# Context projections spread over both layers' experts: 8 in layer 0's, 18 in layer 1's

## The chip, the cores and the metric

The kernel runs on one core of a Trainium2 chip. Its engines are TensorE (PE), VectorE (DVE), ScalarE (ACT), GpSimd (POOL) and SyncE (SP), each with its own instruction stream, and sixteen DMA engines bring the data. The metric is the device time of one execution, in microseconds (us); lower is better. All arithmetic is fp32.

## The reference

Two parts follow each other on 256 tokens of width 1024. The first is two layers (l = 0, 1) of a mixer with three branches and a mixture of 64 experts. The second starts with a mixer of four mLSTM heads and a multi-scale pool, which also sees 256 context tokens, and ends with window attention. Cut to what the change touches:

```python
def first_block(x, ...):
    for l in range(2):
        h = rms_norm(x, norm_mix_g[l]) * (1.0 + sc_m) + sh_m
        x = x + g_m * mixer(h, ...)
        h = rms_norm(x, norm_ffn_g[l]) * (1.0 + sc_f) + sh_f
        x = x + g_f * moe_ffn(h, ...)              # 64 experts and a shared one

def second_block(x, c, ctx, c_ctx, ...):           # layer 0 of it
    shift, scale, gate = jnp.split(silu(c) @ w_mod + b_mod, 3)
    shift_c, scale_c, gate_c = jnp.split(silu(c_ctx) @ w_mod + b_mod, 3)
    hx = rmsnorm(x, g_pre) * (1 + scale) + shift
    hc = rmsnorm(ctx, g_pre) * (1 + scale_c) + shift_c
    ux, uc = hx @ w_in, hc @ w_in                  # q, k, v, o, z (4 heads each), pool in and gate (4 groups each), 16 gates
    qx, kx, vx, gates = mlstm_inputs(ux, ...)      # short_conv of width 3 over q and k
    qc, kc, vc, gates = mlstm_inputs(uc, ...)      # scans over log_i, log_f forward and backward
```

`hc` and `uc` depend on the context and on the modulation vectors alone, not on the first part's result.

## The kernel before

The stages stand one after another in the program. For each layer: a norm and the input projections, the branches, the merge of the branches, the routing, then the experts; after both layers the pools of the second part, its four heads, and its attention. Each stage is a Python generator per engine (`pe_...`, `act_...`, `dve_...`, `pool_...`) that emits the instructions of that engine in a fixed order and yields the event that it waits for. A generator `scan` (L2693 on PE, L2719 on ACT, L2764 on DVE) is woven into the pools by `step(scan)`: each `yield PAUSE` in it, and each count of `pause(n)`, hands control back to the pools for one step.

All weights come through one list, `K.loads`. SP issues it in order (L562 to L577): it waits for the events that a load's place needs, then issues the DMA. Nothing further down the list is issued while it waits. The ring has 11 units of 1 MB (`UNITS`, L20). `places` (L364) assigns the loads of the experts to places: ring slots of two units for `up` (w1 and w3, 2 MB), halves of one unit and the places `x`, `consts` and `last` for `down` (w2, 1 MB), and two `wide` places outside the ring. In layer 0 there are four slots, two halves and place `x` (the memory of `K.gate_a`, which is also that of `K.hc`); in layer 1 three slots and four halves, since `K.hc` holds the normed context there.

The experts take 25 passes (`ORDER`, L29): a pass handles one, two or four experts' tokens, PE multiplies by `up` (L2164), scatters the slots of tokens, multiplies by `down` (L2199) and adds the result to the rows (L2215). `pe_fill` (L2220) adds after a pass of layer 1 one context projection: 16 matmuls of 128x256, whose weights (1 MB of `ab_w_in`) come through the same queue as kind `fill`; `act_fill` copies the 128x512 result into `K.turns`, and `pool_experts` writes it to `ctx_parts` in DRAM. `FILL` lists 18 of them: the pools' input and gate for groups 1 to 3, and v, o and z of the four heads. They are read back before the heads and the pools. The heads' q and k have their context part computed in the second part: `pe_project` (L2990) multiplies by `K.h2`, which holds the context's 256 columns and the tokens' 256 columns, at 128x512.

The context is loaded at the start of layer 1, its norm's sums are made by ACT there (`act_ctx_sums`, L919), and `pool_ctx`, `pe_ctx` (L1747) and `act_ctx` turn it and write `K.hc` beside the branches and the merge of layer 1. Modulation vectors are products of one row with a weight (`pe_mod`, L693): `early_parts` and `EARLY_AT` say which stand behind which input projection. The names `mod2` are those of the second part, and all six (q, j) stand in layer 1's projections.

The scans of the gates run in the pools. For each direction d, DVE makes the scans, PE turns the result (`ecol`, L2714 and L2715, eight small transposes) and ACT copies it into `acol` and `ecol`, which the heads read. ACT starts with direction 1 (L2735) only after the turn of direction 0.

## Time and profile before

| | us |
|---|---|
| three timed runs: median (lowest, highest) | 2498.92 (2497.47, 2500.92) |
| the profiled execution | 2502.77 |
| its span in the profile | 2501.4 |
| layer 0: experts | 408.1 to 871.2 |
| layer 1: start, experts | 871.2, 1278.4 to 1817.3 |
| second part: pools, heads | 1817.3 to 1948.5, to 2212.2 |

The span is the time from the first to the last instruction in the trace; 1.4 us of the profiled execution lie around it. A matmul of fp32 operands appears as two records in the trace, so 16 matmuls are "x32". A row of a timeline tells start, duration, engine, line, operation, output and inputs, and in brackets how long the engine was idle before and for what. "cst", "xT", "ar" and "ring" are places of a weight. PEclk is the granted TensorE clock as a share of full speed. The share of a stage that PE idles is not the price of what it waits for elsewhere: look at each stage by itself.

### The profile page before, as it was taken

Reading aid. Unit: us, or ns where it says so; the run is one execution under the profiler, and the core shown is the slowest. Engines: PE = TensorE matmul, PEld = TensorE weight load, DVE = VectorE, ACT = ScalarE, POOL = GpSimd, SP = SyncE. Lnnn points to the kernel's source line nnn. Section 1 sums busy time; section 2 is a strip of 40 time slices with the busy share of each in tenths; the row PEclk is TensorE's granted clock in tenths of the full one; section 3 lists DMA queues with packets and bytes.
Section 4 is the critical chain, followed back from the end, with each engine's and each line's share of the span. In section 5 each row is a group of like instructions: output and inputs, shape, how many; then the busy total and the mean of one; then the engine's idle time right before and its main releaser. Section 6 shows DMA issues by size and latency. Waiting matters only on the chain.

```text
span 2501.4 us, 29863 instructions
## 1 busy us (share of the span) xinstructions
PE 2334.9 (93%) x11723; PEld 1498.8 (60%) x11723; DVE 848.1 (34%) x2148; ACT 560.1 (22%) x1199; POOL 116.2 (5%) x168
## 2 busy tenths in 40 slices
PE   7999999888888889999999899999997999999998
PEld 4867886344334357678855555555565566654764
DVE  0596523122122115955241221212115233321254
ACT  2224311111111121243111111111123233221264
POOL 4000000000000001100000000000000000001110
PEclk9999999999989999999999999999988999999999
DMA  9644665999999898547569999999951532130500
GB/s 342 244 169 168 253 274 214 421 421 421 421 421 421 352 379 298 180 160 277 232 251 399 414 387 407 415 399 414 388 170 50 164 97 80 68 126 12 190 1 18
DMA packets 196905, 657.70 MB, mean 263 GB/s; under 512 B 13617, under 2 KB 66073, under 8 KB 147089
## 3 DMA queue, kind: packets, MB, share of 16 engines
q1 hardware_dynamic: 191024, 645.33, 66.6%
q0 software_dynamic: 5296, 10.32, 1.3%
q8 instruction: 97, 1.59, 0.3%
q14 instruction: 56, 0.45, 0.1%
q10 hardware_dynamic: 432, 0.01, 0.0%
HBM read 649.58 MB, written 6.04 MB: 262 GB/s over the span
## 4 chain that ended last, share of the span: by engine, by line
PE 82%; DMA 11%; DVE 4%; ACT 1%; issue 1%; SPq 1%; POOL 0%; DVEq 0%; ACTq 0%
PE ps L275 46%; PE ps L2164 12%; PE ps L2199 7%; DMA ring<-in_w 4%; DMA cst<-in_w 3%; PE ps L2215 3%; DMA xT<-in_w 3%; PE ps L1747 2%; PE ps L1205 1%; PE ps L3434 1%; PE ps L693 1%; DVE ar L1344 1%; DMA ring<-in_w_in 1%; PE ps L2825 1%; DMA ring<-in_w_mod 1%
## 5 line engine op out<-in xcount | busy, mean ns | idle before, releaser
L275 PE MATMUL ps<-hT,ring 128*128 128x256 f32 (+2 forms) x2352 | 602.9, 413 | 1.9 <-ACT ar L1565 1.9
L275 PEld LDWEIGHTS ps<-hT,ring 128*128 128x128 f32 (+1 forms) x2352 | 445.2, 192 | 150.4 <-issue 94.4
L2164 PE MATMUL ps<-ring,ar 128*32 128x512 f32 (+2 forms) x1184 | 300.5, 618 | 10.9 <-DMA ring<-in_w 5.6
L2164 PE MATMUL ps<-ar 128*64 128x512 f32 (+1 forms) x864 | 265.5, 615 | 13.3 <-DMA ring<-in_w 13.3
L2199 PE MATMUL ps<-ring,ar 128*32 128x512 f32 (+2 forms) x672 | 182.9, 664 | 49.5 <-DMA cst<-in_w 21.6
L2164 PEld LDWEIGHTS ps<-ring,ar 128*32 128x32 f32 (+2 forms) x1184 | 93.1, 128 | 156.7 <-issue 153.5
L2447 DVE TENSOR_TENSOR ar<-ar,ps 128x256 f32<-128x256 f32 x50 | 21.1, 421 | 472.7 <-ACT ar L2307 472.7
L275 PE MATMUL ps<-ring,ar 128*128 128x512 f32 x320 | 139.8, 593 | 0.9 <-DVE ar L3663 0.9
L2471 DVE SCALAR_TENSOR_TENSOR exact_parts<-ps,ar,exact_parts 128x512 fp32r<-128x512 f32 x100 | 75.1, 751 | 193.1 <-ACT exact_parts L2315 187.3
L2164 PEld LDWEIGHTS ps<-ar 128*64 128x64 f32 (+1 forms) x864 | 74.5, 126 | 98.5 <-issue 97.8
L2315 ACT ACTIVATE exact_parts<-ps,ar 128x512 fp32r<-128x512 f32 x100 | 68.7, 687 | 284.0 <-PE ps L2199 260.6
L2199 PEld LDWEIGHTS ps<-ring,ar 128*32 128x32 f32 (+2 forms) x672 | 53.0, 136 | 126.5 <-issue 122.5
L2199 PE MATMUL ps<-cst,ar 128*64 128x512 f32 (+1 forms) x216 | 113.0, 672 | 9.0 <-DMA xT<-in_w 6.6
L2215 PE MATMUL ps<-exact_parts 128*128 128x512 f32 x400 | 108.6, 411 | 2.1 <-DVE exact_parts L2471 2.1
L275 PE MATMUL ps<-exact_parts,exact_rows 128*128 128x256 f32 x832 | 104.1, 282 | 0.0
L2215 PEld LDWEIGHTS ps<-exact_parts 128*128 128x128 f32 x400 | 71.5, 188 | 54.4 <-issue 33.0
L275 PEld LDWEIGHTS ps<-ring,ar 128*128 128x128 f32 x320 | 60.4, 190 | 72.6 <-issue 70.5
L2307 ACT ACTIVATE ar<-ps 128x256 f32<-128x256 f32 x50 | 19.2, 384 | 376.0 <-PE ps L2164 376.0
L275 PEld LDWEIGHTS ps<-exact_parts,exact_rows 128*128 128x128 f32 x832 | 98.6, 189 | 5.1 <-issue 5.0
L1344 DVE SCALAR_TENSOR_TENSOR ar<-ar,wdw 128x256 f32<-128x256 f32 x240 | 101.0, 492 | 0.0
L275 PE MATMUL ps<-ring,hT 128*128 128x256 f32 (+1 forms) x384 | 100.0, 417 | 0.0
L275 PE MATMUL ps<-ar,ring 128*128 128x256 f32 (+1 forms) x416 | 98.7, 397 | 0.6 <-ACT ar L1699 0.6
(453 smaller groups left out, 2789.2 us busy)
## 6 DMA issues: line engine op xcount, KB each, us to landing
ring<-in_w SPq DMA_DIRECT2D x232, 1024.0 KB, 16.4
ar<-in_w SPq DMA_DIRECT2D x108, 1024.0 KB, 14.5
ring<-in_w_mod SPq DMA_DIRECT2D x36, 2048.0 KB, 11.9
ring<-in_w_in SPq DMA_DIRECT2D x28, 2048.0 KB, 12.2
ring<-in_ab_w_in SPq DMA_DIRECT2D x46, 1024.0 KB, 12.4
cst<-in_w SPq DMA_DIRECT2D x27, 1024.0 KB, 18.7
xT<-in_w SPq DMA_DIRECT2D x17, 1024.0 KB, 20.4
ring<-in_w_out SPq DMA_DIRECT2D x4, 2048.0 KB, 11.2
```

Of the source, the lines that this page charges most:

```text
L275: ins = te.matmul(o, l, r, start=(first and i == 0), stop=(last and i == len(pairs) - 1), skip_group_check=lax)
L693: ins = te.matmul(b[32 * t:32 * t + 32, :], col(2 * t + s), w[:, 2 * t + s, :], start=(s == 0), stop=(s == 1))
L1205: ins = te.matmul(b[:, :], h[:, kk, i * P:(i + 1) * P], w[0][:, kk, :], start=(kk == 0), stop=(kk == 7))
L1344: ins = ve.scalar_tensor_tensor(K.acc[:, c, :], K.hpad[:, c, k:k + 256], tap, K.acc[:, c, :], ALU.mult, ALU.add)
L1747: ins = te.matmul(b[:, 0:256], w[kk // 4][:, kk % 4, k::8], K.merged[:, kk, :], start=(kk == 0), stop=(kk == 7))
L2164: ins = te.matmul(b[cols, :], K.x_b[:, kk, in_pair(p, cols)], weights_up(K, l, r)[:, :, kk, :], start=(kk == 0), stop=(kk == 7))
L2199: ins = te.matmul(b[cols, :], K.t_b[:, j * P + cols.start:j * P + cols.stop], weights_down(K, l, r, j, q), start=(j == 0), stop=(j == 1))
L2215: ins = te.matmul(K.banks[2 * i + q][:, :], K.wT_r[:, p % 2, i * P:(i + 1) * P], part[:, q * 512:(q + 1) * 512], start=False, stop=False, ...
L2315: ac.activation(K.o_hi_r[:, q * 512:(q + 1) * 512], K.ps["down", l, p, q][:, :], ACT.Copy, scale=K.slot[:, p, 1:2]).then_inc(*K.act("o_hi" ...
L2471: ve.scalar_tensor_tensor(K.o_lo_r[:, cols], K.ps["down", l, p, q][:, :], K.slot[:, p, 1:2], K.o_hi_r[:, cols].bitcast(F32), ALU.mult, ALU ...
L2825: ins = te.matmul(b[:, cols], w[:, kk, c * P:(c + 1) * P], h[:, kk, cols], start=(kk == 0), stop=(kk == 7))
L3434: ins = te.matmul(b[:, 0:256], w[:, kk, (n % 2) * P:(n % 2 + 1) * P], hx[:, kk, :], start=(kk == 0), stop=(kk == 7))
```

## The change

- `FILL` gets q and k of the four heads: 26 entries. `FILL_OF` divides them: the first eight (the six pool pieces, q and k of head 0) in layer 0, in passes 3, 4, 5, 8, 10, 12, 15 and 18; the other 18 in layer 1, in the passes that had one before.
- The heads' q and k products become 128x256 (the tokens' columns alone); the context's half comes back from `ctx_parts` by a new load of 512 KB per head (`ctx_qk`), and ACT copies it ahead of each of the four pieces.
- `K.hc` is made in layer 0: the load of the context, `act_ctx_sums` (now at the end of layer 0's projections), `pool_ctx`, `pe_ctx` and `act_ctx` move there, and with them the modulation parts mod2 (0, 0) and (0, 1), behind `qk`. Layer 0's experts then have three slots and four halves, and place `x` is gone. POOL writes `K.hc` to DRAM in layer 0's experts, and a new load `hc` of 1 MB brings it back ahead of layer 1's experts. The sines and cosines in `K.turns` are also written out and brought back.
- The scans: PE's `pause(5)` becomes `pause(7 - d)`, ACT's `pause(4)` becomes `pause(6 - d)`.

```diff
@@ -32,10 +32,12 @@
 CONSTS_PASS = 20
-FILL = [(n, g) for g in range(1, 4) for n in ("pin", "pgate")] + [(n, hd) for hd in range(4) for n in ("v", "o", "z")]
-FILL_COL = {"pin": 5, "pgate": 6, "v": 2, "o": 3, "z": 4}
-FILL_PASS = [p for p in range(3, 24) if ORDER[p] > 1 and p != 13]
-FILL_AT = {p: n for n, p in enumerate(FILL_PASS)}
+FILL = [(n, g) for g in range(1, 4) for n in ("pin", "pgate")] + [(n, hd) for hd in range(4) for n in ("q", "k", "v", "o", "z")]
+FILL_COL = {"pin": 5, "pgate": 6, "q": 0, "k": 1, "v": 2, "o": 3, "z": 4}
+FILL_OF = range(8), range(8, 26)
+FILL_PASS = dict(zip(FILL_OF[0], (p for p in range(2, 24) if ORDER[p] > 2 or p in (3, 10, 22))))
+FILL_PASS |= dict(zip(FILL_OF[1], (p for p in range(3, 24) if ORDER[p] > 1 and p != 13)))
+FILL_AT = [{FILL_PASS[n]: n for n in of} for of in FILL_OF]
@@ -314,6 +317,8 @@
     K.cosT, K.sinT = K.turns[:, 0:256], K.turns[:, 256:512]
+    K.turns_kept = nc.dram_tensor("turns_kept", (P, 512), F32).ap()
+    K.hc_kept = nc.dram_tensor("hc_kept", (P, 2048), F32).ap()
@@ -364,15 +369,13 @@
-    slots = 4 if l == 0 else 3
-    up = {("wide", 0): (-1, None), ("wide", 1): (-1, None), **{("slot", n): (-1, None) for n in range(slots)}}
-    down = {(name, 0): (-1, None) for name in (("x", "consts", "last") if l == 0 else ("consts", "last"))}
-    down |= {("half", u): (-1, None) for u in range(10 - 2 * slots)}
+    up = {("wide", 0): (-1, None), ("wide", 1): (-1, None), **{("slot", n): (-1, None) for n in range(3)}}
+    down = {("consts", 0): (-1, None), ("last", 0): (-1, None), **{("half", u): (-1, None) for u in range(4)}}
...
-        fill = [FILL_AT[p]] if l == 1 and p in FILL_AT else []
+        fill = [FILL_AT[l][p]] if p in FILL_AT[l] else []
@@ -435,7 +438,7 @@
-            ("up", pass_of), ("down", pass_of), ("fill", range(len(FILL)) if l == 1 else ()))]
+            ("up", pass_of), ("down", pass_of), ("fill", FILL_OF[l]))]
@@ -444,9 +447,9 @@
-        if l == 1:
-            wide[1].append(("mod", *early_parts(l)[-1]))
-        first = {"wide": wide, "x": [("merged", l, 0, 7)], "consts": [("ctx_turned", 3)] if l else []}
+        wide[1].append(("mod", *early_parts(l)[-1]))
+        kind, r = K.where[0]["consts"]
+        first = {"wide": wide, "consts": [("used", kind, 0, r)] if l else [("ctx_turned", 3)]}
@@ -477,10 +480,6 @@
     for l in range(LAYERS):
-        if l == 1:
-            K.plan(("ctx",), 1, [(lambda f: f.rearrange("p (i d) -> p i d", i=2),
-                                  I["ctx_2"][0].rearrange("(i p) d -> p i d", p=P))],
-                   (K.cst_place, [("used", "down", 0, K.where[0]["consts"][1])]))
@@ -488,6 +487,9 @@
                     mod(*key)
+        if l == 0:
+            K.plan(("ctx",), 1, [(lambda f: f.rearrange("p (i d) -> p i d", i=2),
+                                  I["ctx_2"][0].rearrange("(i p) d -> p i d", p=P))], (K.cst_place, []))
@@ -500,6 +502,9 @@
         shared(l)
+        if l == 1:
+            K.plan(("hc",), 1, [(lambda f: f, K.hc_kept)],
+                   (K.hc.rearrange("p k t -> p (k t)"), [("merged", 1, 0, 7), ("hc_kept",)]))
@@ -511,8 +516,8 @@
-            if n == "v":
-                ctx_parts(("ctx_head", h), FILL.index(("v", h)), 3)
+            if n in ("q", "v"):
+                ctx_parts(("ctx_qk" if n == "q" else "ctx_head", h), FILL.index((n, h)), 2 if n == "q" else 3)
@@ -718,8 +723,8 @@
     if l == 0:
-        return [("mod", 0, j) for j in range(2, 4)]
-    return [("mod2", q, j) for q in range(2) for j in range(3)]
+        return [("mod", 0, 2), ("mod2", 0, 0), ("mod2", 0, 1), ("mod", 0, 3)]
+    return [("mod2", 0, 2), ("mod2", 1, 0), ("mod2", 1, 1), ("mod2", 1, 2)]
@@ -731,19 +736,19 @@
-EARLY_AT = ("qc", "vc"), ("norm", "va", "ua", "ug", "qc", "qk")
+EARLY_AT = ("qc", "qk", "qk", "vc"), ("ua", "ug", "qc", "qk")
...
-def pe_mod(K, key):
+def pe_mod(K, l, key):
...
-        K.te.wait_ge(*(yield ("cact2",)))
+        K.te.wait_ge(*(yield ("cact2", l)))
@@ -948,8 +953,8 @@
     ac = K.ac
-    ac.wait_ge(*(yield ("scales2", 0)))
-    ac.wait_ge(*(yield ("merged", 1, 0, 7)))
+    ac.wait_ge(*(yield ("ctx_scale",)))
+    ac.wait_ge(*(yield ("merged", 0, 0, 7)))
@@ -1269,17 +1274,15 @@
     ac = K.ac
+    for q in range(2):
+        ac.activation(K.cact2[:, :, q * 16:(q + 1) * 16],
+                      K.cact[:, 1 + q, :].unsqueeze(2).to_broadcast([P, 8, 16]), ACT.Copy).then_inc(*K.act())
+    K.act.also("cact2", l)
...
-        for q in range(2):
-            ac.activation(K.cact2[:, :, q * 16:(q + 1) * 16],
-                          K.cact[:, 1 + q, :].unsqueeze(2).to_broadcast([P, 8, 16]), ACT.Copy).then_inc(*K.act())
-        K.act.also("cact2")
...
-    if l == 1:
-        yield from act_ctx_sums(K)
@@ -1328,6 +1331,8 @@
     yield from act_mod_early(K, l, "vc")
+    if l == 0:
+        yield from act_ctx_sums(K)
@@ -1366,6 +1371,8 @@
         at += 14
+    if l == 1:
+        ve.wait_ge(K.s_turns, 32)
@@ -1392,7 +1399,7 @@
-BEFORE_ROPE = (1, 5)
+BEFORE_ROPE = (1, 3)
@@ -1400,6 +1407,12 @@
     yield from pool_mods(K, l, 0, BEFORE_ROPE[l])
+    if l == 0:
+        gp.wait_ge(*(yield ("sin",)))
+        gp.wait_ge(*(yield ("cos",)))
+        gp.dma_start(K.turns_kept, K.turns[:, :]).then_inc(K.s_turns, 16)
+    else:
+        gp.wait_ge(K.s_turns, 32)
@@ -1691,6 +1704,8 @@
     for br, kept in enumerate((K.gate_a, K.gate_b)):
+        if br == 0 and l == 1:
+            K.ac.wait_ge(*(yield ("hc_kept",)))
@@ -1734,7 +1749,7 @@
             yield from pe_direct(K, l, (3 + br,))
-        if br == 1 and l == 1:
+        if br == 1 and l == 0:
@@ -1763,7 +1778,7 @@
     yield from act_direct(K, l, (3, 4))
-    if l == 1:
+    if l == 0:
@@ -1782,6 +1797,9 @@
             dve_scales2(K, 0)
+        if br == 1 and l == 0:
+            dve_scale(K, K.sc2[0][:, 0, :], K.mods2[0][:, 0, 1, :], K.gpre[0])
+            K.dve.also("ctx_scale")
@@ -1815,7 +1833,7 @@
 def pool_branches(K, l):
-    if l == 1:
+    if l == 0:
@@ -2217,23 +2235,27 @@
-def pe_fill(K, n):
+def pe_fill(K, l, n):
...
-    w = k_major(K.flat["fill", 1, n], 256)
+    w = k_major(K.flat["fill", l, n], 256)
...
-    te.wait_ge(*(yield ("ring", "fill", 1, n)))
+    te.wait_ge(*(yield ("ring", "fill", l, n)))
+    if n == FILL_OF[l][0]:
+        te.wait_ge(*(yield (("ctx_h", 7), ("ring", "hc"))[l]))
...
-    K.pe.also("used", "fill", 1, n)
+    K.pe.also("used", "fill", l, n)
...
+    if n == 0:
+        K.ac.wait_ge(K.s_turns, 16)
@@ -2280,8 +2302,8 @@
         yield from pe_down(K, l, p)
-        if l == 1 and p in FILL_AT:
-            yield from pe_fill(K, FILL_AT[p])
+        if p in FILL_AT[l]:
+            yield from pe_fill(K, l, FILL_AT[l][p])
@@ -2314,8 +2336,8 @@
-        if l == 1 and p in FILL_AT:
-            yield from act_fill(K, FILL_AT[p])
+        if p in FILL_AT[l]:
+            yield from act_fill(K, FILL_AT[l][p])
@@ -2473,14 +2495,25 @@
 def pool_experts(K, l):
+    gp = K.gp
...
-        return
-    for n, p in enumerate(FILL_PASS):
-        if p == CONSTS_PASS:
+        gp.wait_ge(*(yield ("ctx_h", 7)))
+        gp.dma_start(K.hc_kept, K.hc.rearrange("p k t -> p (k t)")).then_inc(K.s_hc, 16)
+        K.ev["hc_kept",] = (K.s_hc, 16)
+    late = l == 1
+    for n in FILL_OF[l]:
+        if late and FILL_PASS[n] >= CONSTS_PASS:
...
-        K.gp.wait_ge(*(yield ("ctx_part", n)))
-        K.gp.dma_start(K.ctx_parts[:, n * 512:(n + 1) * 512], K.turns[:, :]).then_inc(K.s_parts, 16)
-    K.ev["ctx_parts_kept",] = (K.s_parts, 16 * len(FILL))
+            late = False
+        gp.wait_ge(*(yield ("ctx_part", n)))
+        gp.dma_start(K.ctx_parts[:, n * 512:(n + 1) * 512], K.turns[:, :]).then_inc(K.s_parts, 16)
+    if late:
+        yield from late_consts(K)
+    if l == 0:
+        gp.wait_ge(K.s_parts, 16 * len(FILL_OF[0]))
+        gp.dma_start(K.turns[:, :], K.turns_kept).then_inc(K.s_turns, 16)
+    else:
+        K.ev["ctx_parts_kept",] = (K.s_parts, 16 * len(FILL))
@@ -2707,7 +2740,7 @@
     for d in range(2):
-        yield from pause(5)
+        yield from pause(7 - d)
@@ -2738,7 +2771,7 @@
-        yield from pause(4)
+        yield from pause(6 - d)
@@ -2793,7 +2826,7 @@
         te.wait_ge(*(yield ("ring", name, 0)))
-        te.wait_ge(*(yield ("ctx_h", 7)))
+        te.wait_ge(*(yield ("ring", "hc")))
@@ -2944,7 +2977,7 @@
     K.gp.wait_ge(*(yield ("y_turned", 1, 7)))
-    K.gp.wait_ge(*(yield ("ctx_h", 7)))
+    K.gp.wait_ge(*(yield ("ring", "hc")))
@@ -2992,8 +3025,8 @@
         K.te.wait_ge(*(yield ("ring", n, hd)))
-    products(K.te, b[:, :], [(w[:, kk, c * P:(c + 1) * P], K.h2[:, kk, :])
-                             for kk in range(8)]).then_inc(*K.pe("m_ps", n, hd, c, ps=b))
+    products(K.te, b[:, 0:256], [(w[:, kk, c * P:(c + 1) * P], K.h2[:, kk, 256:512])
+                                 for kk in range(8)]).then_inc(*K.pe("m_ps", n, hd, c, ps=b))
@@ -3110,17 +3143,21 @@
     for hd in range(4):
+        ac.wait_ge(*(yield ("ring", "ctx_qk", hd)))
...
-                ac.wait_ge(*(yield ("m_ps", n, hd, c)))
...
-                ac.activation(K.upad[:, :, 1:257], segments(K.ps["m_ps", n, hd, c][:, :]),
+                at = (512 if n == "k" else 0) + c * 256
+                ac.activation(K.upad[:, 0, 1:257], K.flat["ctx_qk", hd][:, at:at + 256], ACT.Copy).then_inc(*K.act())
+                ac.wait_ge(*(yield ("m_ps", n, hd, c)))
+                ac.activation(K.upad[:, 1, 1:257], K.ps["m_ps", n, hd, c][:, 0:256],
...
+        K.act.also("used", "ctx_qk", hd)
```

TensorE, the scans' turns in the pools, before (L2825 is the product of a group's input, the products of L275 with 128x256 are its gate, with 128x512 the pool mix; L2714 opens a turn):

```order
L2825 MATMUL ps<-hT,ring 128x256 x16
L275 MATMUL ps<-ar,ring 128x512 x4
L2714 MATMUL ps<-cst,ar 128x4
...
L2715 MATMUL ps<-cst,ar 128x4
L275 MATMUL ps<-hT,ring 128x256 x16
L2825 MATMUL ps<-hT,ring 128x256 x16
L275 MATMUL ps<-ar,ring 128x512 x4
L2714 MATMUL ps<-cst,ar 128x4
```

The same place after (line numbers are 3 or 33 higher there):

```order
L2858 MATMUL ps<-hT,ring 128x256 x16
L278 MATMUL ps<-ar,ring 128x512 x4
L278 MATMUL ps<-hT,ring 128x256 x16
L2858 MATMUL ps<-hT,ring 128x256 x8
L2747 MATMUL ps<-cst,ar 128x4
...
L2748 MATMUL ps<-cst,ar 128x4
L2858 MATMUL ps<-hT,ring 128x256 x8
L278 MATMUL ps<-ar,ring 128x512 x4
L278 MATMUL ps<-hT,ring 128x256 x16
L2858 MATMUL ps<-hT,ring 128x256 x16
L2747 MATMUL ps<-cst,ar 128x4
```

The first turn moved behind a gate product and half an input product; between the turns stand 40 matmuls of 128x256 and four of 128x512, against 32 and four before.

ScalarE, the end of layer 0's projections and the first instructions of its branches, before:

```order
L1329 ACTIVATE ar<-ps 128x512 x2
L775 ACTIVATE ar<-ps 128x512 x2
L1653 ACT_TABLE_LOAD
L1455 ACTIVATE ar<-ar 128x128 x2
L1552 ACTIVATE ar<-ar 128x384 x2
```

and after:

```order
L1332 ACTIVATE ar<-ps 128x512 x2
L780 ACTIVATE ar<-ps 128x512 x2
L924 ACTIVATE xT,par<-cst 128x1024 x2
L927 ACT_TABLE_LOAD
L927 ACTIVATE par<-par,cst 128x2
L929 ACT_TABLE_LOAD
L929 ACTIVATE par<-par 128x2
L1666 ACT_TABLE_LOAD
L1468 ACTIVATE ar<-ar 128x128 x2
```

The sums of the context, with two table loads of their own, stand ahead of the branches' first exponentials.

TensorE, the start of layer 1, before (L2614 turns the last rows, L693 is a modulation part, L1205 the first input projection), and after:

```order
L2614 MATMUL ps<-cst,hT 128x128 x16
L1122 MATMUL ps<-ar,cst 128x256 x8
L693 MATMUL ps<-ring,ar 32x512 x16
L1205 MATMUL ps<-ring,hT 128x512 x16
L693 MATMUL ps<-ring,ar 32x512 x16
```

```order
L2647 MATMUL ps<-cst,hT 128x128 x16
L1127 MATMUL ps<-ar,cst 128x256 x8
L1210 MATMUL ps<-ring,hT 128x512 x16
L278 MATMUL ps<-hT,ring 128x256 x32
L698 MATMUL ps<-ring,ar 32x512 x16
```

Two modulation parts left this place.

## Rows read from the trace of the kernel before

**Rows 1.** The page's head.

```profile
span 2501.4 us, 29863 instructions
```

**Rows 2.** The page's chain that ended last, by engine.

```profile
PE 82%; DMA 11%; DVE 4%; ACT 1%; issue 1%; SPq 1%; POOL 0%; DVEq 0%; ACTq 0%
```

**Rows 3.** Windows: us, busy (records) by engine, clock, DMA share, GB/s.

```profile
408.10:871.20 463.10, 401.21 (x2422) 187.98 (x2421) 106.69 (x326) 58.31 (x99) 0.00 (x0) 0.93 0.99 411
1278.40:1817.30 538.90, 511.66 (x2995) 292.43 (x2994) 106.70 (x326) 69.06 (x117) 10.28 (x19) 0.98 1.01 403
...
411.60:863.10 451.50, 390.65 (x2360) 183.13 (x2355) 102.83 (x312) 56.93 (x97) 0.00 (x0) 0.93 1.01 418
...
1948.50:2212.20 263.70, 263.65 (x923) 170.96 (x924) 89.84 (x219) 75.82 (x186) 2.96 (x6) 1.00 0.29 97
```

**Rows 4.** PE's waits in layer 0's experts: total, times, longest.

```profile
PE ps L2199 <- DMA cst<-in_w: 17.5, 3, 8.4
PE ps L2164 <- DMA ring<-in_w: 16.8, 5, 5.6
PE ps L2199 <- DMA xT<-in_w: 16.3, 3, 6.9
```

**Rows 5.** PE's longest waits in layer 1's experts, as in rows 4.

```profile
PE ps L2199 <- DMA ring<-in_w: 10.9, 2, 8.2
```

**Rows 6.** Timeline of PE: one context projection in layer 1's experts.

```profile
1435.01 7.17 PE L275 MATMUL ps<-xT,ring 128*128 128x256 f32 x32
```

**Rows 7.** Timeline of PE in the heads: k at 512 columns, then v at 256.

```profile
2014.87 13.89 PE L275 MATMUL ps<-hT,ring 128*128 128x512 f32 x32
...
2043.21 7.07 PE L275 MATMUL ps<-ring,hT 128*128 128x256 f32 x32
```

**Rows 8.** Timeline of DVE in the heads: the normed rows, and the convolution.

```profile
2020.95 1.14 DVE L3234 TENSOR_SCALAR ar<-ar 128x256 f32<-128x256 f32 x4 [1.14 <-ACT ar L3164]
2029.24 1.41 DVE L3171 SCALAR_TENSOR_TENSOR ar<-ps,pmisc,ar 128x512 f32<-128x512 f32 x2 [7.14 <-PE ps L3028]
2030.68 0.49 DVE L3189 TENSOR_SCALAR ar<-ar,pmisc 128x512 f32<-128x512 f32 x1
2031.21 1.54 DVE L3192 SCALAR_TENSOR_TENSOR ar<-ar,pmisc 128x512 f32<-128x512 f32 x2
```

**Rows 9.** Timeline of PE in the pools: both turns and the products behind them.

```profile
1889.28 0.27 PE L2714 MATMUL ps<-cst,ar 4*128 4x4 f32 x1 [7.31 <-DVE ar L2785]
...
1890.22 9.13 PE L275 MATMUL ps<-hT,ring 128*128 128x256 f32 x32
...
1917.26 0.24 PE L2714 MATMUL ps<-cst,ar 4*128 4x4 f32 x1 [7.58 <-DVE ar L2785]
...
1918.18 8.80 PE L275 MATMUL ps<-hT,ring 128*128 128x256 f32 x32
```

**Rows 10.** Timelines of DVE and ACT in the pools: both scans' ends, ACT's start of direction 1.

```profile
1888.54 0.68 DVE L2785 TENSOR_TENSOR ar<-ar 4x512 f32<-4x512 f32 x1
...
1916.44 0.68 DVE L2785 TENSOR_TENSOR ar<-ar 4x512 f32<-4x512 f32 x1
...
1903.62 0.63 ACT L2735 ACTIVATE ar<-ar 4x512 f32<-4x512 f32 x1
```

**Rows 11.** Timeline of PE at the start of layer 1.

```profile
892.92 15.70 PE L1205 MATMUL ps<-ring,hT 128*128 128x512 f32 x32 [4.07 <-DMA ring<-in_w_in]
908.55 3.64 PE L693 MATMUL ps<-ring,ar 128*32 128x512 f32 x32
```

**Rows 12.** Timelines: ACT before layer 0's branches, PE there, ACT's context sums in layer 1.

```profile
163.62 0.60 ACT L775 ACTIVATE ar<-ps 128x512 f32<-128x512 f32 x1 [1.12 <-PE ps L693]
164.23 1.28 ACT L1653 ACT_TABLE_LOAD   x1
...
174.60 0.46 PE L1528 MATMUL ps<-ar,cst 128*128 128x128 f32 x2 [1.80 <-DVE ar L1581]
...
890.08 1.04 ACT L919 ACTIVATE xT<-cst 128x1024 f32<-128x1024 f32 x1
```

More of the change, by code:

```diff
@@ L188, in __init__ @@
         self.items, self.flat, self.after = [], {}, {}
-        self.s_parts = self.sem("ctx_parts_written")
+        self.s_parts, self.s_hc = self.sem("ctx_parts_written"), self.sem("hc_kept")
+        self.s_turns = self.sem("turns_kept")
     def sem(self, name):
@@ L420, in views @@
             return K.wbuf[u].rearrange("p m n -> p (m n)")
-        return {"x": K.gate_a.rearrange("p k t -> p (k t)"), "consts": K.cst_place}[kind]
+        return K.cst_place
     def in_turn(l):
@@ L753, in pe_mod_early @@
     for key in early_at(l, place):
-        yield from pe_mod(K, key)
+        yield from pe_mod(K, l, key)
 def act_mod(K, l, keys):
```

## The prediction

> **What bounds the kernel now.** I read the chain that ended last first: PE carries 82% of it and DMA 11% [rows 2] in a span of 2501.4 us [rows 1]. So a matmul removed counts wherever PE does not wait, and the 11% must be found by stage. The windows by stage show it. In layer 0's experts the DMA share is 1.01 and 418 GB/s flow from the first weight's landing to the last, while PE idles 62 of 463 us [rows 3]. Its waits there are for weights in three kinds of places, 50.6 us together [rows 4]: the queue sets the pace. Layer 1's experts have 18 context projections more, take 538.9 us, PE is busy 512 of them [rows 3], and the longest kind of wait is 10.9 us [rows 5]: PE sets the pace, the queue close behind. In the heads PE is busy 263.65 of 263.7 us at DMA share 0.29 [rows 3], so there PE alone counts. In the pools PE waits twice for a scan [rows 9].
>
> **Layer 0's experts: eight projections more.** One costs 7.17 us of PE [rows 6], eight 57.4 us, and one load of 1 MB each. A megabyte (1.049 million bytes) at 418 GB/s [rows 3] is 2.5 us. With place `x` gone, one megabyte less of the experts' weights can land ahead, so 9 loads more weigh on the queue: 9 x 2.5 = +22.5 us. That is the lower end, in which all PE work falls into waits that exist. The upper end is PE's whole time, +57. Between them stands the other layer, which is the same stage with 18 of them: (538.9 - 463.1) / 18 = 4.2 us for one [rows 3], 8 x 4.2 = 33.7, and 2.5 for the lost place: **+36**. I take this, because both engines end up close: PE alone would need 538.9 - 10 x 7.17 = 467 us, the queue 463.1 + 22.5 = 485.6. Two engines that near to each other, coupled by 16 MB of places, lose something to each other in both directions; a queue that waits for a place once doesn't get that time back.
>
> **Layer 1's experts** keep 18 in the same passes: 0. The new load `hc` stands ahead of their weights, one megabyte where the mean of the queue is not full, 0 to 2.5: +1.
>
> **Heads.** q and k of a head are two products of 16 matmuls. One took 13.89 us at 512 columns [rows 7], at 256 columns v takes 7.07 [rows 7]. 8 x (13.89 - 7.07) = -54.6 us, all on the path since PE has no wait there. What could be late next: (a) The normed rows, DVE L3234, end at 2022.1; PE now reaches L3028, which reads them, at 2014.87 + 7.07 = 2021.9. The 7.14 us that DVE waited [rows 8] are used up to within 0.2, a wait of about 0.2 in three heads. (b) The convolution. Each of the four pieces goes through one padded tile: two ACT copies of half the size of one that takes 0.60 [rows 12], and DVE's 0.49 + 1.54 [rows 8]: at most 3.2 us, against a PE piece of 3.5. It keeps up, with a late last piece. I give back 2.3 us in all: **-52.3**. The context's part of q and k is a 512 KB load per head at a share of 0.29: hidden.
>
> **Scans turned later.** PE waited 7.31 and 7.58 us, and the 16 matmuls behind each wait took 9.13 and 8.80 us instead of 7.07 [rows 9], the clock having been at its lower level after the wait. If both waits go, this returns too: 14.9 + 2.1 + 1.7 = 18.7. Turn 0: its scan ends at 1889.2 [rows 10], and PE now has 7.1 + 3.5 us of products ahead of it, more than the 7.31 it waited. No wait. Turn 1: the scan of direction 1 starts on ACT only after turn 0, one copy and half an input product; from ACT's start to DVE's end are 1917.1 - 1903.6 = 13.5 us [rows 10], behind about 4.3 us of product and copy: 18 us after turn 0. PE has 3.5 + 3.6 + 7.1 + 7.1 = 21.3 us of work between its turns. It fits with 3 us to spare: **-18.7**; the other end is -9 (the second wait stays).
>
> **Layer 1's start.** Two modulation parts of 3.64 us leave it [rows 11] and enter layer 0, where the DMA share leaves room: neutral. The first input projection waited 4.07 us for its weight, and took 15.7 us [rows 11] where two products of its size elsewhere take 13.9 [rows 7]. The loads of the context and of four MB of modulation no longer stand ahead of that weight. The normed rows, not the weight, then set its start, about 2 us after PE is free. -2 for the wait, -1 for the clock: **-3** (0 to -4).
>
> **The context in layer 0.** PE's part only changes layer. ACT's sums now stand ahead of the branches' first exponentials: two squares of 1.04, two table loads of 1.28, two small ones, 5.3 us [rows 12]. ACT was idle 1.1 us there, PE already waits 1.80 us for what comes of it [rows 12], so the delay reaches PE: 0 to +7, taken **+4**.
>
> The Trainium skill ("ScalarE: Activation LUTs", "What ACT_TABLE_LOAD costs") adds a drain of 1.38 us to each switch, which would make this term 2.8 us larger. The trace disagrees: the copy that ends at 164.22 is followed by the load at 164.23 [rows 12].
>
> **Sum.** 36 + 1 - 52.3 - 18.7 - 3 + 4 = -33.0. The profiled execution took 2502.77 us (span 2501.4 and 1.4 around it), so 2469.8 in its terms. It stands 3.85 above the median of the timed runs, 2498.92, from which I count: **2466 us**.
>
> **Rivals.**
> A, only the queue is paid in layer 0: +22.5 instead of +36, 2452. For it: PE's 50.6 us of waits nearly hold 57 us of projections, and less waiting means less time at the lower clock (0.93 against 0.98 in layer 1 [rows 3]). Against: the projections stand after fixed passes, the waits where the weights are late. The Trainium skill ("TensorE: Matmul & The Clock Gate", "Loop structure matters more than you think") says that waits for DMA between products lower the clock and work in their place keeps it; by that rule the answer is this rival. Layer 1 agrees in clock, but its 4.2 us for one does not.
> B, nearly all of PE's time is paid, +55: 2485. For it: the waits gather where no projection is; the queue stops when PE is behind and 16 MB are full. Against: layer 1's 4.2.
> C, the second scan's wait only moves: its chain is longer than 21.3 us because ACT's copies of the pools now stand between, and the wait of 7.6 and the slow product stay: -33 + 9.3, 2475.
> D, slower than before. A projection's weight stands in the single queue ahead of experts' weights and its place comes free only when PE has done that projection; if PE then waits for the next weight, its 7.17 and the queue's 2.5 add up rather than overlap: 8 x 9.7 + 2.5 = 80 instead of 36, -33 + 44 = +11: 2510. It decides from a price of (36 + 33 - 2.5) / 8 = 8.3 us for one, twice what layer 1 shows.
> E, the heads' convolution can't follow: a piece above 3.5 us holds PE. At 4.5 us a piece it is 16 x 1.0 = 16 us given back: 2482.
>
> **How the numbers follow.** Forecast (2456 to 2476) 0.46; A 0.17; B 0.12; C 0.13; D 0.04; E 0.08. The range takes in A, C, E and B: 2448 to 2487. A run of this kernel can tell 0.2%, 5 us, from no change. Faster by more (below 2494): all but D and the upper edge of B, 0.93. Within: 0.03. Slower: 0.04.
>
> **What would show it.** Layer 0's experts at 499 us, PE's waits there down from 50.6 to about 30, DMA share still near 1, clock up. Layer 1's experts at 539 within 3. A head's q and k at 7.07 us for 16 matmuls, four heads in 211 us instead of 264. No wait for a scan on PE. In layer 0's branches a wait some 4 us longer in front of L1528. The prediction is wrong if layer 0's experts are outside 485 to 520 us, or if a new wait stands in the heads.

## The result

| | us | |
|---|---|---|
| before: median of 5 (lowest, highest) | 2498.92 | (2496.69, 2501.88) |
| changed: median of 5 | 2484.6 | (2482.38, 2486.48) |
| ratio, 95% interval | 0.9942 | 0.9927 to 0.9956 |
| predicted | 2466 | 2448 to 2487 |

The kernel got faster by 14.3 us, less than half of the 33 that were forecast. By the profiled spans, 2501.4 [rows 1] and 2482.4, it is 19.0. Of the 4.7 us between the two figures 4.4 are the draw of the two profiled executions: that of before lay 3.85 us above its median, that of after 0.6 below.

The changed kernel's head line and its chain that ended last, by engine, beside [rows 1, 2]:

```profile
span 2482.4 us, 30440 instructions
...
PE 81%; DMA 10%; DVE 4%; ACT 2%; SPq 1%; issue 1%; ACTq 0%; DVEq 0%
```

The shares hardly move. The windows by stage tell where the time went. Windows of the changed kernel (us; busy time and records of PE, weight load, DVE, ACT, POOL; clock; DMA share; GB/s):

```profile
0.00:170.50 170.50, 155.80 (x723) 106.44 (x723) 72.51 (x158) 39.52 (x65) 35.06 (x61) 0.98 0.86 300
170.50:350.40 179.90, 166.91 (x897) 139.82 (x894) 107.94 (x241) 66.54 (x166) 15.93 (x19) 0.97 0.61 221
350.40:421.80 71.40, 69.11 (x339) 59.92 (x338) 23.60 (x97) 14.67 (x27) 0.00 (x0) 1.00 0.37 149
421.80:929.10 507.30, 445.01 (x2675) 234.65 (x2674) 106.77 (x326) 63.11 (x107) 4.89 (x9) 0.95 1.00 407
929.10:945.10 16.00, 3.91 (x16) 3.25 (x17) 1.72 (x5) 4.36 (x8) 0.00 (x0) 0.57 1.01 374
945.10:1086.00 140.90, 137.91 (x608) 95.04 (x608) 66.25 (x127) 27.21 (x48) 12.21 (x13) 0.99 0.64 227
1086.00:1256.90 170.90, 162.53 (x876) 136.35 (x877) 107.64 (x248) 57.00 (x149) 6.86 (x12) 0.98 0.58 211
...
1328.30:1867.50 539.20, 510.38 (x2996) 291.67 (x2994) 106.77 (x326) 69.08 (x117) 10.28 (x19) 0.98 0.99 398
1867.50:1980.10 112.60, 105.81 (x426) 77.64 (x425) 47.55 (x74) 39.58 (x71) 2.93 (x3) 0.94 0.40 129
1980.10:2482.40 502.30, 493.04 (x2100) 335.78 (x2100) 181.80 (x451) 173.21 (x443) 34.42 (x43) 1.00 0.29 99
```

Beside the same stages of before:

| stage | before | after | moved | forecast |
|---|---|---|---|---|
| layer 0: start, projections | 163.5 | 170.5 | +7.0 | +7.3 (parts moved in) |
| layer 0: branches and merge | 171.8 | 179.9 | +8.1 | +2.1 (moved in), +4 |
| both layers: norm, routing | 73.1, 73.2 | 71.4, 71.4 | -3.5 | 0 |
| layer 0: experts | 463.1 | 507.3 | **+44.2** | +36 |
| from layer 0's last matmul to the norm | 10.1 | 16.0 | **+5.9** | 0 |
| layer 1: projections | 149.3 | 140.9 | -8.4 | -7.3 (moved out), -3 |
| layer 1: branches and merge | 174.3 | 170.9 | -3.4 | -2.1 (moved out) |
| layer 1: experts | 538.9 | 539.2 | +0.3 | +1 |
| second part: pools | 131.2 | 112.6 | -18.6 | -18.7 |
| second part: heads and the rest | 552.9 | 502.3 | -50.6 | -52.3 |

The pools and the heads came out as worked out. By the spans 14 us of the 33 are missing, and two rows hold as much: layer 0's experts (8.2) and the gap behind them (5.9). The other differences cancel.

PE's waits in layer 0's experts, changed kernel (total, times, longest):

```profile
PE ps L2182 <- DMA ar<-in_w: 25.1, 6, 10.2
PE ps L2182 <- DMA ring<-in_w: 16.7, 3, 12.9
PE ps L2217 <- DMA ring<-in_w: 7.7, 1, 7.7
```

49.5 us for weights, against 50.6 of [rows 4]; the forecast had said about 30. PE got 57 us of matmuls more (its busy time grew by 44) and waits as long as before. But it waits for something else: before, two of three kinds were `down` weights (L2199), now the two largest are `up` weights (L2182) in the wide places and the slots.

### The profile page after: what moved, and what is told of

Read it like the earlier page. It is cut to its first block, busy times and chain, and to the rows that moved or that the text cites. A ratio compares the mean times of both kernels' runs of the same rounds, so it can differ in the third digit from the quotient of the medians.

```text
span 2482.4 us, 30440 instructions
## 1 busy us (share of the span) xinstructions
PE 2319.5 (93%) x11979; PEld 1540.5 (62%) x11979; DVE 846.2 (34%) x2149; ACT 568.9 (23%) x1227; POOL 122.6 (5%) x179
## 4 chain that ended last, share of the span: by engine, by line
PE 81%; DMA 10%; DVE 4%; ACT 2%; SPq 1%; issue 1%; ACTq 0%; DVEq 0%
PE ps L278 45%; PE ps L2182 12%; PE ps L2217 6%; DMA ring<-in_w 4%; PE ps L2233 3%; PE ps L1762 2%; DMA ar<-in_w 2%; DMA cst<-in_w 2%; SPq L582 1%; PE ps L1210 1%; PE ps L698 1%; PE ps L2858 1%; PE ps L3471 1%; DVE ar L1349 1%; DMA ring<-in_w_in 1%
## 5 line engine op out<-in xcount | busy, mean ns | idle before, releaser
L278 PE MATMUL ps<-hT,ring 128*128 128x256 f32 (+2 forms) x2352 | 546.7, 388 | 3.2 <-ACT ar L1578 1.9
L2182 PE MATMUL ps<-ring,ar 128*32 128x512 f32 (+2 forms) x1056 | 290.7, 613 | 44.2 <-DMA ar<-in_w 25.1
L2182 PE MATMUL ps<-ar 128*64 128x512 f32 (+1 forms) x992 | 291.4, 608 | 1.5 <-DMA ar<-in_w 1.5
L2182 PEld LDWEIGHTS ps<-ring,ar 128*32 128x32 f32 (+2 forms) x1056 | 91.6, 128 | 194.2 <-issue 188.3
L278 PE MATMUL ps<-xT,ring 128*128 128x256 f32 x576 | 128.9, 382 | 0.0
L2182 PEld LDWEIGHTS ps<-ar 128*64 128x64 f32 (+1 forms) x992 | 81.9, 125 | 75.6 <-issue 72.8
L278 PEld LDWEIGHTS ps<-xT,ring 128*128 128x128 f32 x576 | 108.0, 190 | 27.6 <-DVE exact_parts L2493 5.0
L2217 PE MATMUL ps<-cst,ar 128*64 128x512 f32 (+1 forms) x216 | 106.4, 638 | 5.5 <-DMA ring<-in_w 3.0
## 6 DMA issues: line engine op xcount, KB each, us to landing
ring<-in_w_out SPq DMA_DIRECT2D x4, 2048.0 KB, 10.3
```

The source lines that it names most:

```text
L278: ins = te.matmul(o, l, r, start=(first and i == 0), stop=(last and i == len(pairs) - 1), skip_group_check=lax)
L2182: ins = te.matmul(b[cols, :], K.x_b[:, kk, in_pair(p, cols)], weights_up(K, l, r)[:, :, kk, :], start=(kk == 0), stop=(kk == 7))
L2217: ins = te.matmul(b[cols, :], K.t_b[:, j * P + cols.start:j * P + cols.stop], weights_down(K, l, r, j, q), start=(j == 0), stop=(j == 1))
```

## The experiments

All ratios are to the kernel before, measured beside it. "Experts" is the window of layer 0's experts in the one profiled execution, the ratio comes from all timed ones. The changed kernel with four slots and the combined one have the same instructions in that stage and differ by 4.7 us there, so a few us of a window are not shown by it alone. The three kernels without projections, loads or products leave work out and compute other results.

| kernel | ratio (95%) | median | experts, layer 0 |
|---|---|---|---|
| changed | 0.9942 (0.9927 to 0.9956) | 2484.6 | 507.3 |
| later turns alone | 0.9918 (0.9904 to 0.9932) | 2481.55 | 462.9 |
| changed, turns undone | 1.0006 (0.9996 to 1.0015) | 2502.7 | 506.6 |
| changed, no projections in layer 0 | 0.9860 (0.9842 to 0.9877) | 2466.1 | 492.3 |
| changed, their loads only | 0.9930 (0.9911 to 0.9949) | 2484.71 | 512.7 |
| changed, their products only | 0.9849 (0.9831 to 0.9866) | 2465.12 | 487.2 |
| before, three slots in layer 0 | 1.0093 (1.0077 to 1.0110) | 2527.27 | 492.0 |
| changed, four slots in layer 0 | 0.9882 (0.9866 to 0.9899) | 2473.69 | 496.8 |
| changed, loads held at layer 1's start | 0.9899 (0.9882 to 0.9915) | 2476.87 | 507.3 |
| changed, heads at 512 columns | 1.0122 (1.0105 to 1.0139) | 2534.39 | |
| combined | 0.9848 (0.9834 to 0.9861) | 2462.34 | 501.5 |
| later turns and one held load | 0.9908 (0.9892 to 0.9925) | 2477.3 | |

### The scans: alone, and undone

```diff
     for d in range(2):
-        yield from pause(5)          # PE
+        yield from pause(7 - d)
...
-        yield from pause(4)          # ACT
+        yield from pause(6 - d)
```

> The kernel before with nothing but the scans' later turns (pause 7 - d on PE, 6 - d on ACT). My theory: both waits on PE in the pools (7.3 and 7.6 us) go and the products behind them return to 7.07 us; from the first row norm of the second part to the first turn of the tokens 96 us instead of 115, the whole 19 us faster than before, about 2480, and as fast as or faster than the changed kernel (2484.6), since all the rest of the change together gives nothing. Rival: the projections moved out of the heads carry a gain of their own, then this kernel is slower than the changed one by 5 us or more.

> The changed kernel with the scans' turns where they were (pause 5 and 4). Theory: the scans' gain is independent of the rest, both waits return, 18 to 19 us slower than the changed kernel, 2502 to 2504, which is the kernel before within 0.2%: all the rest of the change together gives nothing. Rival: with the narrow heads or other loads the waits are shorter, then less than 14 us.

The turns alone give 0.9918, the changed kernel 0.9942, and the changed kernel without them is the kernel before (1.0006). So the measured gain is the gain of two numbers in `pause`. All the rest together, the narrow heads among it, gave nothing: what the heads gained, layer 0's experts lost. Both expectations held. With the turns undone, PE waits for the two scans again:

```profile
PE ps L2747 <- DVE ar L2818: 14.9, 2, 7.6
```

Timeline of PE in the pools of the changed kernel; the answers to [rows 9]:

```profile
1939.55 3.62 PE L2858 MATMUL ps<-hT,ring 128*128 128x256 f32 x16
1943.10 0.22 PE L2747 MATMUL ps<-cst,ar 4*128 4x4 f32 x1
...
1957.59 7.07 PE L2858 MATMUL ps<-hT,ring 128*128 128x256 f32 x32
1964.59 0.22 PE L2747 MATMUL ps<-cst,ar 4*128 4x4 f32 x1
...
1968.72 7.07 PE L278 MATMUL ps<-hT,ring 128*128 128x256 f32 x32
```

Neither turn has a wait in brackets, and the gate product that follows the second takes 7.07 us, no longer 8.80: the clock's share of the gain is there too. 21.5 us lie between the turns, as estimated (21.3).

### What the eight projections cost, split

```diff
# no projections: neither planned, loaded nor multiplied in layer 0
-        if p in FILL_AT[l]:
+        if l == 1 and p in FILL_AT[l]:
# loads only: 2 instead of 16 matmuls each
+                                      for kk in range(8 if l == 1 else 1)])
# products only: no load, the weights read from K.hc
+    w = k_major(K.flat["fill", l, n], 256) if l == 1 else K.hc
```

> The changed kernel without the eight context projections in layer 0: no products, no loads, no copies there (their eight parts of ctx_parts are filled with other data, the rest is computed from them). What stays is the lost megabyte of place x, and 16 places. Theory: layer 0's experts take 466 us (463 before, 507 changed), so the projections cost 41 of the 44 us, whole 2443. Rival, the lost place is the cause: 475 to 490 us, whole 2455 or more. Also: the second stop of PE at the start of layer 1 (5.3 us) stays if it comes from the loads in flight there, since those are the same.

> The changed kernel with all eight loads of the projections in layer 0 but 2 instead of 16 matmuls for each (their results are wrong sums). Theory: the queue alone is paid: 9 MB more than before at 2.5 us, experts 463 + 22 + some 3 = 485 to 490 us, whole 2463 to 2468. Rival, a queue that stops for places whatever PE does: over 495 us.

> The changed kernel with the eight projections' 16 matmuls each in layer 0, read from the normed context itself, and none of their loads (results wrong). PE gets 57.4 us of work more, the queue only the lost megabyte. If products fall into PE's 51 us of waits: experts 466 to 480 us, whole 2443 to 2457. If the waits are elsewhere than the projections, products cost nearly all their time less what the higher clock gives back: 495 to 505 us, whole 2475 to 2484. I expect the middle, 482: waits that come after a projection shrink, the queue gains nothing by it.

My theory fell at the first of them, and at the second. Without any projection the stage takes 492.3 us, 29 more than before and not 3. With the loads only it takes 512.7, not 485 to 490: the loads add 20.4. The products without loads take 5.1 off, where I expected 482; both together add 15.0. Windows of layer 0's experts, without projections, with loads only, with products only:

```profile
422.30:914.60 492.30, 398.66 (x2419) 188.22 (x2418) 106.75 (x326) 58.39 (x99) 0.00 (x0) 0.91 0.96 397
```

```profile
423.10:935.80 512.70, 411.68 (x2451) 195.71 (x2450) 106.80 (x326) 63.18 (x107) 4.89 (x9) 0.91 0.99 403
```

```profile
424.20:911.40 487.20, 441.74 (x2675) 232.69 (x2674) 106.76 (x326) 63.08 (x107) 4.87 (x9) 0.96 0.99 406
```

PE's two longest kinds of wait, without projections, then with products only:

```profile
PE ps L2182 <- DMA ar<-in_w: 58.0, 9, 12.6
PE ps L2182 <- DMA ring<-in_w: 24.3, 4, 12.9
```

```profile
PE ps L2182 <- DMA ring<-in_w: 18.0, 3, 12.8
PE ps L2182 <- DMA ar<-in_w: 16.7, 4, 8.2
```

PE is busy 43 us longer in the third window than in the first, and the stage is 5 us shorter. The granted clock went from 0.91 to 0.96, and PE's waits for weights shrank from 82 to 35 us. The products put on top of the loads do the same (507.3 for 512.7). The medians of the whole show none of these 5 us (2465.12 against 2466.1, 2484.6 against 2484.71). So it is shown that 57 us of matmuls were free here, and not that they made the kernel faster; eight loads were not free. The Trainium skill ("TensorE: Matmul & The Clock Gate", "Loop structure matters more than you think") says that a long wait for DMA between matmuls lowers the clock, and that back-to-back matmuls keep it up. The trace agrees with 0.96 against 0.91.

The rival in the first of these expectations was the lost place. It was right: 492.3 us, just above the 475 to 490 that it said.

### The lost place

```diff
# the kernel before, in places()
-    slots = 4 if l == 0 else 3
+    slots = 3
-    down = {... (("x", "consts", "last") if l == 0 else ("consts", "last"))}
+    down = {... ("consts", "last")}
```

> The kernel before with layer 0's experts in three slots and four halves and without place x, as the changed kernel has them; no projection is there. In up weights that is five places instead of six (10 MB, not 12). Theory: the missing sixth place, and not the projections, makes the larger part of the 44 us: the removal of the projections left 29 us of them. Layer 0's experts here 489 to 494 us (463 before), the whole 26 to 31 us slower, 2525 to 2532. Rival, the queue loses only the megabyte that is not ahead: 466 us and 2503.

492.0 us where it was 463.1, with not one projection: +28.9 us, and 1.0093 in all. The stage is as expected, the whole 23.7 us slower by the medians where I expected 26 to 31. Its window, and its longest kind of wait:

```profile
410.60:902.60 492.00, 398.29 (x2419) 188.30 (x2418) 106.72 (x326) 58.38 (x99) 0.00 (x0) 0.91 0.94 389
```

```profile
PE ps L2164 <- DMA ar<-in_w: 57.9, 8, 12.5
```

The DMA share is 0.94 where [rows 3] show 0.99: the queue stands still at times. What SP waits for in front of a load, in this stage before and in this kernel, says on what: the time for which it waits until the `up` products (L2164) have freed a place doubles, while that for the `down` products (L2199) falls from 179.5 to 68.0.

```profile
SPq L577 <- PE ps L2164: 132.6, 23, 14.3
SPq L577 <- PE ps L2164: 264.2, 24, 24.7
```

A pass of four experts needs four `up` places of 2 MB. With six such places (two wide, four slots) two are left to load ahead into, with five only one. SP waits in order, so everything behind the blocked `up` load waits too. The next kernel asks whether the division decides or the size:

```diff
+FILL_PASS = dict(zip(FILL_OF[0], (6, 7, 9, 10, 13, 16, 19, 20)))
...
+    slots = 4 if l == 0 else 3
+    up = {("wide", 0): ..., ("wide", 1): ..., **{("slot", n): ... for n in range(slots)}}
+    down = {("consts", 0): ..., ("last", 0): ..., **{("half", u): ... for u in range(10 - 2 * slots)}}
```

> The changed kernel with four slots and two halves in layer 0 (six places for up weights, four for down weights and projections, 16 MB as in the changed kernel) and the eight projections behind passes that handle one or two experts: 6, 7, 9, 10, 13, 16, 19, 20. Theory: with the sixth up place the queue stops for places hardly at all, and the price falls to the DMA's: experts 490 us instead of 507, the whole 15 to 18 us faster than the changed kernel, 2467 to 2470. Rival: the number of megabytes counts, not their division; then 505 us and 2484 as before.

The same 16 MB, divided into six `up` places and four others: 496.8 us, 10.5 less than the changed kernel, and the DMA share is 1.01. A pass of four experts and a projection can't share four places, so the projections had to move behind passes of one or two experts; what that alone does was not tried, and so the 10.5 us are not shown to be the division's alone. The whole is 0.9882, faster than the changed kernel by 0.6% (10.9 us by the medians, 15 by the ratios; I had expected 15 to 18, and 490 us for the stage).

```profile
422.30:919.10 496.80, 448.67 (x2675) 233.10 (x2674) 106.68 (x326) 63.14 (x107) 4.89 (x9) 0.97 1.01 412
```

So the sixth place gives back 10.5 us here, not 28.9, and the stage is still 33.7 us longer than before. The two costs overlap: eight projections cost 15.0 us where five places already stop the queue, and 33.7 where it doesn't stop. What they cost there is mostly bytes. DMA in this stage, before and in this kernel, and the part of the latter that POOL issues:

```profile
DMA packets 26149, 190.40 MB, mean 411 GB/s; under 512 B 2896, under 2 KB 2896, under 8 KB 2958
DMA packets 36671, 204.82 MB, mean 412 GB/s; under 512 B 3200, under 2 KB 11392, under 8 KB 13350
q0 software_dynamic: 720, 2.36, 1.2%
```

14.4 MB more at an equal rate. 8.4 are the projections' weights, 2.4 POOL's copies to and from DRAM, 1.0 the megabyte that no longer lands ahead, and the rest are mostly first loads of layer 1, which start before PE's last matmul of the stage. The first three, 11.8 MB, make 28 us at the 418 GB/s of [rows 3], as an estimate, of the 33.7.

### The gap behind the experts

Timeline of PE, changed kernel, and the instruction packets of DMA in 926 to 945 us (packets, MB, share of 16 engines):

```profile
935.40 0.45 PE L2647 MATMUL ps<-cst,hT 128*128 128x128 f32 x1 [6.30 <-issue]
941.16 3.46 PE L2647 MATMUL ps<-cst,hT 128*128 128x128 f32 x15 [5.31 <-issue]
```

```profile
q8 instruction: 3, 0.05, 1.1%
```

Before, there was one stop of 6.0 us. The second, in the middle of sixteen transposes that wait for nothing, was new. The DMA share of this gap was 1.01.

The first stop has a name in the trace. In front of L2647 PE's sequencer has a branch, which leads around the blocks for overflow, once per layer (durations in ns: shortest, median, longest; first and last start in us). On PE it takes 6.7 us in layer 0 and 6.4 in layer 1, on ACT 0.05:

```profile
L2550 PEldq COMPARE_BRANCH  x2: 6447/6568/6690, 928.5 to 1867.1; - x2
L2550 ACTq COMPARE_BRANCH  x2: 45/48/50, 929.6 to 1868.2; - x2
```

The experiment holds loads back:

```diff
+        if l == 1:
+            K.after["mod2", 0, 2, 0] = [("y_turned", 0, 7)]
```

> The changed kernel with the first modulation load of layer 1 held back until PE has turned the last rows of layer 0, and so the loads behind it. In the changed kernel PE stops twice there, 6.3 and 5.3 us, in front of L2647 and after its first matmul, with four to eight MB in flight. If the loads in flight cause the second stop it goes, from PE's last matmul of the experts to the first row norm 10 us instead of 16, the whole 5 us faster, 2480. If the place of the code does, it stays and the whole is within 2 us of 2485.

PE in that kernel, and the window of the gap:

```profile
932.54 0.45 PE L2649 MATMUL ps<-cst,hT 128*128 128x128 f32 x1 [3.07 <-ACT ar L1280]
935.90 3.46 PE L2649 MATMUL ps<-cst,hT 128*128 128x128 f32 x15 [2.90 <-issue]
```

```profile
929.50:939.90 10.40, 3.95 (x17) 3.31 (x17) 1.78 (x5) 4.39 (x9) 0.00 (x0) 0.61 0.02 7
```

The gap is 10.4 us, not 16.0, at a DMA share of 0.02. The first stop now ends with ACT's work, the second is 2.9 instead of 5.3. The branch itself takes 3.4 us in layer 0, where the loads are held, and 6.7 in layer 1, where they are not:

```profile
L2552 PEldq COMPARE_BRANCH  x2: 3370/5048/6727, 928.9 to 1857.7; - x2
```

The other runs bear this out. The 13 kernels hold 26 such branches. With the DMA share at 1.00 or more while they run, 22 of them take 5.9 to 7.8 us; the three with the loads held back (this one, and one each in the last two kernels below), at shares of 0.03 to 0.05, take 3.4 to 3.6. The 26th, at 0.66, is in the combined kernel below. So loads in flight lengthen the branch. The whole gained more than the 5 us that I expected, 7.7 by the medians; 2.7 us of it lie in layer 1's branches, where the waits are the same and the granted clock is 1.00, not 0.98.

The second stop follows the loads in its length, but not in whether it comes. Behind layer 0's experts six variants of the changed kernel, itself among them, have it with loads in flight, 4.7 to 5.9 us long; in the one with four slots it joins the first, to 11.5. With the loads held it takes 2.9, here and in the combined kernel. The kernel before and its three variants don't have it, nor has the changed kernel with the projections' loads only, where the DMA share of the gap was 1.04 as well. Why is open.

### The heads

```diff
-    products(K.te, b[:, 0:256], [(w[:, kk, c * P:(c + 1) * P], K.h2[:, kk, 256:512])
+    products(K.te, b[:, :], [(w[:, kk, c * P:(c + 1) * P], K.h2[:, kk, :])
```

> The changed kernel with the heads' q and k products at 512 columns again, the context's columns among them (they are not used). Theory: PE alone paces the heads in both, so 16 products a head times 8 pairs cost 6.82 us each, 8 x 6.82 = 54.6 us less what the narrow version lost in waits, 50 to 55 us slower than the changed kernel, 2535 to 2540. If the convolution's chain already held the narrow version by much, less than 45.

ACT then copies the tokens' half of each product. Windows of the four heads, changed kernel and this one:

```profile
1980.10:2193.00 212.90, 210.71 (x924) 170.24 (x925) 90.14 (x220) 77.25 (x202) 2.95 (x6) 1.00 0.40 133
```

```profile
1982.90:2246.60 263.70, 263.70 (x923) 170.55 (x924) 89.93 (x219) 78.39 (x202) 2.95 (x6) 1.00 0.32 107
```

50.8 us; the whole was 49.8 slower by the medians, 45 by the ratios. Of the 54.6 on paper 3.8 are missing; two kinds of wait of the narrow version hold 2.2 of them:

```profile
PE ps L278 <- ACT ar L3158: 1.3, 3, 0.4
PE ps L3061 <- DVE ar L3271: 0.9, 3, 0.3
```

### Put together

Four parts on the changed kernel: four slots with the other passes; the held loads of layer 1; `ctx_pool` 1 held until PE has turned the rows of layer 1; the context's sums between ACT's two copies of `vc`.

```diff
         ac.activation(K.vc[:, i, :], ...)
+        if l == 0 and i == 0:
+            yield from act_ctx_sums(K)
...
-        K.after[key] = [("ctx_parts_kept",)]
+        K.after[key] = [("ctx_parts_kept",)] + ([("y_turned", 1, 7)] if key == ("ctx_pool", 1) else [])
```

> The changed kernel with four things: four slots and the eight passes 6, 7, 9, 10, 13, 16, 19, 20 in layer 0 (11 us by its own run), the loads of layer 1's start held back until PE has turned the rows (8 us), the same for the load ctx_pool 1 at the start of the second part (PE stops 5.9 us there with three to four loads in flight: 0 to 3 us), and the context's sums on ACT between the two copies of vc in layer 0, where ACT idles 6 us, instead of ahead of the branches (4 to 6 us of the branches' 8 us). If they add up: 24 us faster than the changed kernel, 2458 to 2463, and below both kernels. Rival: the stops and waits move to the next place, then 2468 or more. By stage: layer 0's branches 174 to 176 us instead of 180.

2462.34, ratio 0.9848 (0.9834 to 0.9861): 39 us below the kernel before measured beside it, below both kernels. Layer 0's branches and merge take 173.1 us instead of 179.9. The stages are a little short of the sum: its experts take 501.5, not 496.8, and the gap is 13.2 with one stop of 8.9. The branch takes 6.57 us there, starting 0.5 ahead of the stop, and 2.9 more pass behind it. For the branch the hold came too late: two loads of 2 MB each (`in_w_in`) were issued at 907.3, ahead of the held one, and the DMA share while the branch ran was 0.66. In front of the second part, at a share of 0.05, it takes 3.39:

```profile
L2553 PEldq COMPARE_BRANCH  x2: 3387/4978/6570, 916.0 to 1848.4; - x2
```

What of this needs no projection moved:

> The kernel before with the later turns and with the load ctx_pool 1 held until PE has turned the last rows of layer 1: what of the combined kernel's parts can be had without moving the projections, the heads or the context. PE's stop there was 5.3 us before and 2.8 in the combined kernel. Theory: 2 to 4 us faster than the later turns alone, ratio to before 0.990 to 0.991, so the move of the projections with the sixth up place is worth about 14 us (0.9848 for the combined kernel). Rival: the stop doesn't follow the loads, then ratio 0.992 as with the turns alone.

```profile
PE ps L2614 <- ACT hT L2603: 3.1, 1, 3.1
```

The stop before the second part (5.7 us by "issue" with the turns alone) is now a wait of 3.1 for ACT. The ratio, 0.9908, lies 0.1% below 0.9918, inside both intervals; the stop is shown, its worth in the whole is not. Against the combined kernel's 0.9848 it leaves 0.6%, 15 us, for the moved projections with the sixth `up` place, the narrow heads and the rest.

## Why the prediction was right or wrong

- **What bounds the kernel.** Right: the queue in layer 0's experts, PE in layer 1's and in the heads.
- **Layer 0's experts.** The step that failed is the price of the lost place: one megabyte of head start, 2.5 us. By itself it costs 28.9 (492.0 for 463.1). With it failed the line drawn through two layers, which put all of (538.9 - 463.1) us on 18 projections, 4.2 each, and added 2.5 for the place: the layers differ in projections and in places. The runs give 28.9 for the place and 15.0 for eight projections on top of it, or, in the other order, 33.7 for the projections with six `up` places and 10.5 for the lost one, there with other passes. In the first order two large errors of opposite sign hide each other (2.5 for 28.9, 33.7 for 15.0), and it is luck that the sum missed by 8 only. That the second order gives the very 33.7 of the forecast is no support for the line: bytes explain most of it. Whether the place matters in layer 1, where the DMA share is 1.01 [rows 3], no run tried. The measure was wrong too: SP's waits point at how many of the next pass's `up` weights could be on their way.
- **The queue's lower end**, nine loads and 22.5 us, left out what POOL writes and reads, 2.4 MB in the stage, 5.6 us at 418 GB/s as an estimate. With the queue running without a stop the eight projections cost 33.7, well above it.
- **The signs I named.** The stage lay within 485 to 520 us and no large wait stands in the heads, so these did not warn. PE's waits did: 49.5 us for about 30. They said that the queue ran later than forecast.
- **Rival A** had the better mechanism for the projections (PE's work is hidden, the queue is paid: 15.0 us measured, 20 for the eight loads) and lacked the place. **B** named 2485 us for the whole, and 2484.6 came, by luck: its reason, that PE's time is paid, is wrong (the products without loads cost nothing), and its +55 for the stage is 11 too many. **D**'s sum of both did not occur.
- **The gap behind the experts** (+5.9) was no term of mine, although the row of before had 6.0 us of "issue" there, at a DMA share of 1.04 by its window. It had no releaser, and I took it as fixed. The stop that grew by 5.3 us of these is the second one, whose cause is open.
- **Heads**: -50.6 for -52.3. The wait for DVE at L3061 is 0.3 in three heads, as said (0.2); ACT's copy holds three more by 0.4. E did not occur.
- **Scans**: -18.6 for -18.7, both waits and the clock's part. C did not occur.
- **Layer 1's start**: -8.4 for -10.3. The wait for the weight went, and one of 2.2 us for ACT's normed rows took its place, as said. The clock's part did not come: the first input projection takes 15.67 us, where it took 15.70.
- **Norm and routing**: -3.5 for 0. The granted clock there was 1.00, not 0.98, in both layers. In layer 0 it was 1.00 with the turns alone as well, and 0.98 in the changed kernel without projections, so this is not shown to be the change's doing.
- **The context on ACT**: +6.0 for +4. The wait came earlier than said: a new one of 4.7 us in front of L1442, while the wait in front of L1528, now L1541, fell from 1.8 to 1.2. The two table loads are there, back to back with their neighbours, and show no drain. The first of them:

```profile
173.34 1.28 ACT L927 ACT_TABLE_LOAD   x1
174.64 0.29 ACT L927 ACTIVATE par<-par,cst 128x2 f32<-128x2 f32 x1
```

- **The base.** I took differences off one profiled execution and subtracted them from a median. 4.7 of the 19.0 us by the spans are not in the medians.

## What to carry to other kernels

Before a cost is scaled from one stage to another, list all that differs between the two; here a buffer that went away in passing cost 29 us by itself. In a queue that waits in order, count first the places of the largest item in the widest step; only where these suffice do the megabytes set the price, and then all of them, the copies out to DRAM too. Two costs that both make the same queue late overlap: price them together, or say in which order. Test each half of a change by itself: here two numbers made the whole gain and the large half gave nothing until its buffers were divided otherwise.

## What the runs showed of the hardware

- In a stage bound by weights, 57 us of matmuls put between the waits cost nothing (487.2 us with them, 492.3 without, both without their loads), with the granted clock at 0.96 instead of 0.91.
- A branch behind the experts took PE 5.9 to 7.8 us in all 22 cases with the DMA share at 1.00 or more, and 3.4 to 3.6 us in all three at 0.03 to 0.05; in the changed kernel the same line took ACT 0.05 us. With the loads held, the gap was 10.4 us instead of 16.0, and before the second part a stop of 5.7 us became a 3.1 us wait for ACT. That the time goes into the fetch of the code behind the branch fits the instruction packets in that window, and was not shown. The second stop behind it, 5.3 us in the changed kernel and 2.9 with the loads held, is unexplained.
